# Modulation loaded by quarters, two product groups advancing behind each, index and taps over both row halves

## The chip, the cores and the metric

The kernel runs on one core of one Trainium2 chip, in one launch. The metric is the device time of that core in microseconds (us): median 2101.46 of 3 runs (2100.26 to 2109.39). The core has five engines that run programs of their own and meet by semaphores: TensorE (PE, with its weight loads PEld), VectorE (DVE), ScalarE (ACT), GpSimd (POOL) and SyncE (SP), which here only issues DMAs. TensorE writes to PSUM: two pairs of banks `ps` for the large products, four banks `pm` for everything small.

## The reference, cut to what matters

256 tokens, model width 2048, everything fp32. Two layers follow each other; the change touches the start of the first and two small places.

```
mod = silu(c) @ ada_w + ada_b               # 2048 x 6144: shift, scale, gate
h = rms_norm(x, norm_g) * (1 + scale) + shift
proj = h @ w_in                             # 2048 x 9296: 19 groups of up to 512 columns
q, k = rope(rms_norm(...)); qi, ki = rope(...)        # 16 index heads of 64 channels
score = sum_h relu(qi . ki * 64**-0.5) * wi           # the index; top 64 keys per query
o_a = attention over the selected keys; o_r = gated linear recurrence
x = x + gate * (concat(o_a, o_r) @ w_out)
# second layer: input product, implicit filter (its taps: h3 @ w4, 64 channels deep),
# attention, two branches, output product, feed-forward network
```

`h` depends on the shift and scale of its own channel only: channel tile k (128 channels) of `h` needs columns 128k to 128k+127 of each. No row of `h @ w_in` is complete before all 16 channel tiles are in.

## The kernel before, in words

**The large products.** A weight matrix comes in groups of 512 columns. A group has four chunks (1.049 MB: four channel tiles of 128 x 512 fp32) of two parts each; a part is two channel tiles. Parts are numbered through the whole kernel (`Gemm.part`, L128): group 0 of the input product has parts 0 to 7, group 1 has 8 to 15. For each part ScalarE rounds the weights to `w_hi` (`high`, L390), VectorE subtracts for the remainder `raw_lo` (`low`, L401), and TensorE does 12 matmuls of 512 columns: two channel tiles, two token halves, three products of high and low halves (`multiply_group`, L411). `raw` is a ring of four chunks, `w_hi` a ring of four parts; SyncE issues a chunk when the parts that had its place are multiplied (`stream`, L375). So ScalarE and VectorE can be up to three parts ahead of TensorE. Group j accumulates in bank pair j % 2 of `ps` and must wait until group j - 2 was read out.

**Other work by parts.** Everything else is a generator that yields the part from which it may go on, or the microseconds that a step is guessed to cost (`Spare`, L134). Each engine calls its generators behind each part, some with a budget per part. Constants such as INDEX_AT, GATE_AT and TAPS_AT (L76 to L93) set the parts; ScalarE and VectorE go LEAD = 3 parts behind TensorE's own number, which is about the same moment.

**The modulation.** Shift and scale are 8 groups of 512 columns of ada_w, in order of columns: four groups of shift, four of scale. Each comes in four chunks into the same ring `raw` (SyncE, L2198 to L2203; `ada_free`, L369). TensorE multiplies the column silu(c) with chunks 0 and 2 and one quarter of chunk 3, nine matmuls of 512 columns (`ps<-raw,c_sig`; an fp32 matmul is two instructions in the trace); VectorE multiplies and adds chunk 1 and the rest of chunk 3 into `mod_part` (L1149, L1151), and a matmul with ones adds its partitions (`ps<-mod_part,ones`). ScalarE copies the row to SBUF (L1857), TensorE turns it to columns by four 1x1 products per group (`ps<-ones,mod_row`). When all eight are turned, VectorE makes `mod_cols` and `g_col` (L1163, L1164), ScalarE and VectorE the high and low halves of `h` from the transposed rows (`tile_of_first` L1785 reading the PSUM bank, `low_of_first` L962), and the first product begins. VectorE does small work between its steps in this stretch (`before_products`, L1099): it scales the rows of x, prepares the lower bound of the forget gate (maximum, exponentials, reciprocals) and computes the sines and cosines of the rotation. Three of the eight units of transposes of `hbuf` are made in this stretch, five between the first parts.

**Index and taps.** The index multiplies 16 heads in 8 units j for each token half t (`index`, L642). A unit takes one bank and two matmuls; both read the same 64 partitions, the lower half for even j and the upper for odd j. One unit goes behind each part, from parts 90 and 104 on. ScalarE applies the relu (L1954), VectorE weights and adds (L1268). The taps of the second layer's filter (L756 to L762) are 8 matmuls of 512 columns with 64 partitions, two behind each part; t picks the half, and the first four are t = 0.

Of the kernel before, what the change touches and what calls it, by code (L numbers as in the profile page):

```python
# [9 lines left out]
F32 = mybir.dt.float32  # L10
# [42 lines left out]
ROWS_TURNED = 4  # L53
ADA_PE = 1
# [22 lines left out]
GATE_AT = [12 + 22 * i // 5 for i in range(4 * ADA_GATE)]  # L77
# [28 lines left out]
class Gemm:  # L106


    chunks = 0
    groups_before = 0  # L110

    def __init__(self, sources, k_tiles, groups, columns=None):
        self.sources, self.cpg, self.groups, self.columns = sources, k_tiles // CK, groups, columns
# [14 lines left out]
    def part(self, j, n=0):  # L128
        return self.n0 + self.parts * j + n

# [26 lines left out]
def build(nc, a, out):  # L157
    Gemm.chunks = Gemm.groups_before = 0
    ctx = ExitStack()
    with ctx:  # L160
# [44 lines left out]
        sn_rope = sb("sn_rope", [P, 5, 2 * TT * 96], F32, st)  # L205
        st.close()
# [37 lines left out]
        mod_row = sb("mod_row", [P, 2 * D], F32, st)  # L244
        mod_part = sb("mod_part", [P, 2, GW], F32, st)
# [21 lines left out]
        lb, lb_tmp = proj[:, :, I_Q:I_Q + A_W], xtmp[:].rearrange("p a n -> p (a n)")  # L267
# [48 lines left out]
        mod_bank = ps[1][:, 1]  # L316
# [7 lines left out]
        g_in = Gemm([(w1v, 0)], KT, len(GROUPS_IN), GROUPS_IN)  # L324
# [9 lines left out]
        landed = [sem(f"landed{i}") for i in range(RING)]  # L334
        ada_used = sem("ada_used")
# [29 lines left out]
        def multiplied(eng, gm, j):  # L365
            eng.wait_ge(mm_done, gm.part(j + 1))
            return ps[pair_of(gm, j)]

        def ada_free(sp, g, c):  # L369

            if c != 1:
                sp.wait_ge(ada_used, 3 * (g - 1) + {0: 1, 2: 2, 3: 3}[c])
            if c % 2:
                sp.wait_ge(mod_parts, 2 * (g - 1) + 1 + c // 2)

        def stream(sp, gm, beside=None):

            for j in range(gm.groups):
                for c in range(gm.cpg):
                    k = gm.c0 + gm.cpg * j + c  # L380
                    if k < RING:
                        ada_free(sp, n_ada, k)
                    else:
                        sp.wait_ge(mm_done, PARTS * (k + 1 - RING))
                    v, o = gm.source(j)
                    sp.dma_start(raw[:, k % RING, :, 0:gm.width(j)], v[c][:, :, o:o + gm.width(j)]).then_inc(landed[k % RING], 16)
# [3 lines left out]
        def high(act, gm, j, n):  # L390
# [3 lines left out]
            if p % PARTS == 0:  # L394
                act.wait_ge(landed[k % RING], 16 * (n_ada + k // RING + 1))
# [15 lines left out]
        def multiply_group(pe, gm, j, stat, before=None, beside=None):  # L411

            pair = pair_of(gm, j)
            if gm.g0 + j >= 2:
                evacuated(pe, gm, j - 2)
            kt = gm.cpg * CK
            for n in range(gm.parts):
                if before is not None:
                    before(n)
                p = gm.part(j, n)  # L420
                pe.wait_ge(lo_done, p + 1)
                hi = w_hi[:, p % HRING]
                lo = raw_lo[:, (p // PARTS) % RING, HT * (p % PARTS):HT * (p % PARTS) + HT]
                for i in range(HT):
                    k = HT * n + i
                    x_hi, x_lo = stat(k, j)
                    for t in range(TT):
                        tok = slice(t * P, t * P + P)
                        for q, (l, r) in enumerate(((x_hi, hi), (x_hi, lo), (x_lo, hi))):
                            mm = nc.tensor.matmul(ps[pair][:, t, 0:gm.width(j)], l[:, tok], r[:, i, 0:gm.width(j)],  # L430
                                                  start=(k == 0 and q == 0), stop=(k == kt - 1 and q == 2))
                mm.then_inc(mm_done, 1)
                if beside is not None:
                    beside.step(p)
# [74 lines left out]
        def _(pe):  # L509
# [27 lines left out]
            pe.wait_ge(sig("c_silu"), 1)  # L537
            for g in range(n_ada):
                pe.wait_ge(sig("mod_read"), g + 1)
                for c in (0, 2, 3):  # L540
                    pe.wait_ge(landed[c], 16 * (g + 1))
                    for k in range(CK if c < 3 else ADA_PE):
                        m = mm(ps[g % 2][0:1, 0, :], c_sig[:, CK * c + k:CK * c + k + 1], raw[:, c, k],
                               start=(c == 0 and k == 0), stop=False)
                    m.then_inc(ada_used, 1)
                pe.wait_ge(mod_parts, 2 * g + 2)
                mm(ps[g % 2][0:1, 0, :], ones[:, 0:1], mod_part[:, g % 2], start=False, stop=True).then_inc(sig("mod_sum"), 1)
                if g >= 1:
                    pe.wait_ge(sig("mod_read"), g + 2)
                    for j in range(4 * (g - 1), 4 * g):  # L550
                        mm(mod_bank[:, j:j + 1], mod_row[0:1, j * P:j * P + P], ones[0:1, 0:1])
                if g >= ROWS_TURNED and g < ROWS_TURNED + 3:
                    pe.wait_ge(sig("h1_rows"), 1)
                    turn_unit("h1", hbuf, g - ROWS_TURNED)
            pe.wait_ge(sig("mod_read"), n_ada + 2)
# [1819 lines left out]
```

## Time and profile before

| | |
|---|---|
| runs | 2100.26, 2101.46, 2109.39 us |
| profiled execution | 2106.29 us, span 2104.5 us |
| TensorE busy | 2058.0 us, 98% |
| VectorE, ScalarE, GpSimd busy | 1302.7, 927.1, 383.0 us |
| mean granted TensorE clock | 0.986 of 2.4 GHz |
| DMA | 408.47 MB, mean 194 GB/s; 353 and 344 GB/s in the first two fortieths |

The busy time of TensorE says that it has work in its pipe, not that it is at its peak: ends of matmuls are modelled, so the durations of neighbours overlap; the distance between two starts is what one costs. "Idle before" is the time an engine stood still ahead of an instruction and what ended it. The granted clock is a share of 2.4 GHz; 0.5 is the lower of its two levels.

### The profile page before, as it was taken

The numbers are of one execution on the slowest core, as the hardware profiler recorded it, in microseconds if no ns is written. First come the engines' busy times: TensorE is split into PE (matmuls) and PEld (weight loads), VectorE is DVE, ScalarE is ACT, GpSimd is POOL, SyncE is SP. The second block draws the span as 40 slices with busy tenths as digits, with TensorE's granted clock in tenths as the row PEclk, the third lists the DMA queues.
The fourth block names the chain that finished last, engine by engine and source line by source line (L and its number), as shares of the span: only waits on it lengthen the run. The fifth ranks groups of instructions, "written<-read, shape, count | busy, mean of one in ns | idle before, by whom it ended". The sixth has DMA issues, their size and how long they took to land.

```text
span 2104.5 us, 23568 instructions
## 1 busy us (share of the span) xinstructions
PE 2058.0 (98%) x9245; PEld 1623.4 (77%) x9245; DVE 1302.7 (62%) x1651; ACT 927.1 (44%) x1224; POOL 383.0 (18%) x588
## 2 busy tenths in 40 slices
PE   6989999999999999999999999999999999999999
PEld 1268787777887888786788888888888888878887
DVE  4857667798666678865765666554544544444443
ACT  1165523455654544354454434554444444433332
POOL 0000002999999950000000000000000000000000
PEclk9999989999999999999999999999999999999999
DMA  9967557555565675554435555555555555546554
GB/s 353 344 236 249 199 185 220 180 171 164 171 213 196 200 231 180 160 163 130 138 129 186 187 198 180 180 194 187 191 188 186 194 186 194 194 166 199 186 195 160
DMA packets 205683, 408.47 MB, mean 194 GB/s; under 512 B 10826, under 2 KB 12163, under 8 KB 204931
## 3 DMA queue, kind: packets, MB, share of 16 engines
q1 hardware_dynamic: 190480, 376.07, 54.1%
q10 hardware_dynamic: 13332, 24.40, 3.4%
q0 software_dynamic: 1760, 6.49, 1.5%
q8 instruction: 73, 1.20, 0.2%
q14 instruction: 38, 0.31, 0.0%
HBM read 404.83 MB, written 2.10 MB: 193 GB/s over the span
## 4 chain that ended last, share of the span: by engine, by line
PE 91%; DVE 6%; DMA 2%; issue 1%; ACT 0%; ACTq 0%; SPq 0%; DVEq 0%
PE ps L430 81%; PE pm L511 6%; DMA raw<-in_ada_w 2%; DVE raw_lo L408 1%; PE ps L511 1%; PE pm L523 1%; DVE mod_part L1151 1%; PE pm L575 1%; PE pm L888 0%; DVE gate L1182 0%; DVE xtmp L1351 0%; DVE sc_i L1268 0%; DMA rows_b<-in_hgrn_norm_g 0%; DVE proj L1328 0%; PE pm L710 0%
## 5 line engine op out<-in xcount | busy, mean ns | idle before, releaser
L408 DVE TENSOR_TENSOR raw_lo<-raw,w_hi 128x1024 fp32r<-128x1024 f32 (+1 forms) x648 | 799.9, 1238 | 597.6 <-ACT w_hi L399 589.0
L399 ACT ACTIVATE w_hi<-raw 128x1024 fp32r<-128x1024 f32 (+1 forms) x648 | 680.1, 1050 | 821.0 <-PE ps L430 796.3
L430 PE MATMUL ps<-w_hi,h_hi 128*128 128x512 f32 (+1 forms) x2336 | 941.3, 403 | 12.5 <-DVE raw_lo L408 6.4
L430 PE MATMUL ps<-w_hi,h_lo 128*128 128x512 f32 (+1 forms) x2336 | 912.5, 391 | 0.0
L430 PE MATMUL ps<-raw_lo,h_hi 128*128 128x512 f32 (+1 forms) x2336 | 911.2, 390 | 0.0
L430 PEld LDWEIGHTS ps<-w_hi,h_hi 128*128 128x128 f32 x2336 | 442.8, 190 | 117.3 <-issue 13.0
L430 PEld LDWEIGHTS ps<-raw_lo,h_hi 128*128 128x128 f32 x2336 | 443.3, 190 | 93.3 <-issue 7.7
L430 PEld LDWEIGHTS ps<-w_hi,h_lo 128*128 128x128 f32 x2336 | 442.2, 189 | 93.4
L2265 POOL TENSOR_TENSOR proj<-proj 128x128 f32<-128x128 f32 x264 | 177.8, 679 | 12.9
L2265 POOL TENSOR_TENSOR proj<-proj,w1T 128x128 f32<-128x128 f32 x165 | 102.8, 631 | 11.4 <-DMA proj<-in_z 4.2
L430 PE MATMUL ps<-w_hi,hid_hi 128*128 128x512 f32 x256 | 100.6, 393 | 2.0 <-DVE raw_lo L408 2.0
L430 PE MATMUL ps<-raw_lo,hid_hi 128*128 128x512 f32 x256 | 100.3, 392 | 0.0
L430 PE MATMUL ps<-w_hi,hid_lo 128*128 128x512 f32 x256 | 100.2, 391 | 0.0
L2244 POOL DMA_DIRECT2D proj<-in_z x22 | 14.1, 645 | 344.4 <-DVEq L1246 338.7
L511 PE MATMUL ps<-raw,c_sig 128*1 128x512 f32 x144 | 70.2, 638 | 6.7 <-DMA raw<-in_ada_w 6.5
L430 PEld LDWEIGHTS ps<-w_hi,hid_hi 128*128 128x128 f32 x256 | 48.3, 189 | 12.3 <-DVE raw_lo L408 2.2
L511 PEld LDWEIGHTS ps<-raw,c_sig 128*1 128x1 f32 x144 | 11.5, 87 | 59.5 <-issue 47.0
L430 PEld LDWEIGHTS ps<-w_hi,hid_lo 128*128 128x128 f32 x256 | 48.5, 189 | 10.1
L430 PEld LDWEIGHTS ps<-raw_lo,hid_hi 128*128 128x128 f32 x256 | 48.4, 189 | 10.0
L1182 DVE SCALAR_TENSOR_TENSOR gate<-proj,c_sig,gate 128x512 f32<-128x512 f32 x64 | 49.1, 767 | 1.9
L2265 POOL TENSOR_TENSOR proj<-h3T,proj 128x128 f32<-128x128 f32 x66 | 48.9, 742 | 0.0
L1151 DVE SCALAR_TENSOR_TENSOR mod_part<-raw,c_sig,mod_part 128x512 f32<-128x512 f32 x48 | 36.0, 750 | 10.2 <-DMA raw<-in_ada_w 8.6
(308 smaller groups left out, 1183.5 us busy)
## 6 DMA issues: line engine op xcount, KB each, us to landing
raw<-in_w_in SPq DMA_DIRECT2D x140, 1024.0 KB, 5.2
raw<-in_w_ffn_gate SPq DMA_DIRECT2D x44, 1024.0 KB, 5.2
raw<-in_w_ffn_up SPq DMA_DIRECT2D x44, 1024.0 KB, 5.2
raw<-in_w_ffn_down SPq DMA_DIRECT2D x44, 1024.0 KB, 5.2
raw<-in_ada_w SPq DMA_DIRECT2D x32, 1024.0 KB, 7.7
raw<-in_w_out SPq DMA_DIRECT2D x32, 1024.0 KB, 5.2
proj<-in_ada_w ACTq DMA_DIRECT2D x16, 1024.0 KB, 5.3
raw<-in_w_br_hyena SPq DMA_DIRECT2D x8, 1024.0 KB, 5.2
```

The source lines that it names most:

```text
L399: nc.scalar.activation(w_hi[:, p % HRING, :, 0:gm.width(j)], raw[:, k % RING, e:e + HT, 0:gm.width(j)], ACT.Copy).then_inc(hi_done, 1)
L408: nc.vector.tensor_tensor(raw_lo[:, k % RING, e:e + HT, 0:gm.width(j)], raw[:, k % RING, e:e + HT, 0:gm.width(j)], w_hi[:, p % HRING, :, 0 ...
L430: mm = nc.tensor.matmul(ps[pair][:, t, 0:gm.width(j)], l[:, tok], r[:, i, 0:gm.width(j)], start=(k == 0 and q == 0), stop=(k == kt - 1 and ...
L511: return nc.tensor.matmul(o, l, r, start=start, stop=stop, **kw)
L523: i = nc.tensor.transpose(b[:, ((k % 2) * TT + t) * P:((k % 2) * TT + t + 1) * P], src[:, t, k * P:k * P + P], ident[:])
L575: i = nc.tensor.transpose(b[:, o:o + P], src[:, t, h * HD:h * HD + HD], ident[:])
L1151: i = v.scalar_tensor_tensor(mod_part[:, g % 2], raw[:, c, k], w_, mod_part[:, g % 2], ALU.mult, ALU.add)
L1182: x = v.scalar_tensor_tensor(acc, gate_raw[i % 2][:, k], c_sig[:, CK * c + k:CK * c + k + 1], acc, ALU.mult, ALU.add)
L2244: pool.dma_start(z_k[e % 2][half * HID:half * HID + HID], z.partition_broadcast(HID)).then_inc(sig(f"z_in{e % 2}"), 16)
L2265: g.tensor_tensor(o, x, y, op).then_inc(sig("sum_step"), 1)
```

## The change

1. **Order of ada_w.** The 8 groups are loaded as shift 0, scale 0, shift 1, scale 1, ...: each pair (a quarter) is enough for four channel tiles of `h`. They go to four buffers of their own in `proj`, so `raw` is free for w_in. Behind each odd group's chunks 0 and 1 SyncE issues one chunk of w_in for group 0 and one for group 1.
2. **Who sums.** TensorE now takes chunk 0 and half of chunk 2 (six matmuls), VectorE the other ten steps of sixteen instead of seven. The sums are in banks of `pm`.
3. **Two product groups together.** Parts 0 to 15 alternate between groups 0 and 1 by chunk. Behind quarter q come parts 4q to 4q + 3, worked off while the next quarter is loaded and summed (`early_part`). The last quarter's four come after all.
4. **Transposes.** All 8 units are made ahead of the third group's sums and copied to SBUF (`h1_raw`); `tile_of_first` reads them there.
5. **Moved.** The rotation's angles go from the first stretch to groups 2 and 3 (budget 1.6 per part); the 16 chunks of the gate row start at parts 22 to 78 instead of 12 to 78; the reciprocals are cut in four.
6. **Index and taps.** A unit pair takes two banks, and the four matmuls alternate the halves; the pair stands behind every second part, one part later than the first of the two stood. The taps go in the order n, t.

```diff
-GATE_AT = [12 + 22 * i // 5 for i in range(4 * ADA_GATE)]
+GATE_AT = [22 + 56 * i // 15 for i in range(4 * ADA_GATE)]
...
     def part(self, j, n=0):
+        if self.together and j < 2 and n < self.parts:
+            return self.n0 + 2 * PARTS * (n // PARTS) + PARTS * j + n % PARTS
         return self.n0 + self.parts * j + n
...
+        mod_row = sb("mod_row", [P, 2, GW], F32, st)
+        mod_part = sb("mod_part", [P, 2, GW], F32, st)
...
+        h1_raw = sb("h1_raw", [P, KT, SEQ], F32, st)
...
+        ada_raw = [proj[:, 1, o:o + CK * GW].rearrange("p (k n) -> p k n", k=CK) for o in (A_Q, A_V, R_Q, R_I)]
...
         def ada_free(sp, g, c):
-            if c != 1:
-                sp.wait_ge(ada_used, 3 * (g - 1) + {0: 1, 2: 2, 3: 3}[c])
-            if c % 2:
-                sp.wait_ge(mod_parts, 2 * (g - 1) + 1 + c // 2)
+            if c % 2 == 0:
+                sp.wait_ge(ada_used, 2 * (g - 1) + 1 + c // 2)
+            if c:
+                sp.wait_ge(mod_parts, 3 * (g - 1) + c)
...
+            for g in range(n_ada):
+                o = D * (g % 2) + GW * (g // 2)
                 for c in range(RING):
+                    if g:
+                        ada_free(sp, g, c)
+                    sp.dma_start(ada_raw[c], ada_v[:, CK * c:CK * c + CK, o:o + GW]).then_inc(ada_landed[c], 16)
+                    if g % 2 and c < 2:
+                        load(sp, g_in, c, g // 2)
...
+            def early_part(p):
+                n = 2 * (p // 4) + p % 2
+                pe.wait_ge(sig("first_lo"), n + 1)
+                multiply_part(pe, g_in, p % 4 // 2, n, halves)
             for g in range(n_ada):
+                q = g // 2 - 1
...
+                mods = bank(pe, ("mods", q), "v") if q >= 0 and g % 2 == 0 else None
+                sums = bank(pe, ("mod", g), "a")
+                row_sums(g, 0, CK, sums)
+                if q >= 0:
+                    if g % 2 == 0:
+                        turn_modulation(q, mods)
+                    elif g < n_ada - 1:
+                        early_part(4 * q + 2)
+                row_sums(g, 2, PE_C2, sums)
+                if q >= 0 and g % 2 and g < n_ada - 1:
+                    early_part(4 * q + 3)
+                pe.wait_ge(mod_parts, 3 * g + 3)
+                mm(sums[0:1, :], ones[:, 0:1], mod_part[:, g % 2], start=False, stop=True).then_inc(filled, 1)
+                if q >= 0:
+                    if g % 2 == 0:
+                        early_part(4 * q)
+                        early_part(4 * q + 1)
+                    elif g == n_ada - 1:
+                        early_part(4 * q + 2)
+                        early_part(4 * q + 3)
+            q = n_ada // 2 - 1
+            turn_modulation(q, bank(pe, ("mods", q), "v"))
+            for p in range(2 * g_in.parts - 4, 2 * g_in.parts):
+                early_part(p)
...
-                    for j in range(IDX_H // 2):
-                        yield INDEX_AT[1 + t] + j
+                    for j in range(0, IDX_H // 2, 2):
+                        yield INDEX_AT[1 + t] + j + 1
-                        b = bank(pe, ("ix", t, j), "a")
-                        part = slice(IDX_D * (j % 2), IDX_D * (j % 2) + IDX_D)
+                        b = [bank(pe, ("ix", t, j + r), "a") for r in range(2)]
                         for q in range(2):
-                            m = mm(b[:, q * SEQ:q * SEQ + nk], qiT[part, j // 2 * 2 + q, t * P:t * P + P], kiT[part, 0:nk])
-                        m.then_inc(filled, 1)
+                            for r in range(2):
+                                part = slice(IDX_D * r, IDX_D * r + IDX_D)
+                                m = mm(b[r][:, q * SEQ:q * SEQ + nk], qiT[part, j + q, t * P:t * P + P], kiT[part, 0:nk])
+                                if q:
+                                    m.then_inc(filled, 1)
...
-                    t, n = i // 4, i % 4
+                    t, n = i % TT, i // TT
...
+                for c, k0 in ((1, 0), (2, PE_C2), (3, 0)):
...
+                    if q >= 0 and g % 2 == 0:
+                        if c == 1:
+                            columns_of(q)
+                        else:
+                            low_of_first(2 * q + c - 2)
+                    if g % 2 and c == 3:
+                        for p in range(4 * (g // 2), 4 * (g // 2) + (2 if g == n_ada - 1 else 4)):
+                            low_of(p)
+                    early.step(g, 3.0 if g < 2 else 1.2)
...
+                p = 4 * (g // 2)
+                high_of(p)
+                high_of(p + 1)
+                if g < n_ada - 1:
+                    high_of(p + 2)
+                    high_of(p + 3)
+                read_row(g)
+                act.wait_ge(sig("mod_ready"), g // 2 + 1)
+                for u in (g - 1, g):
+                    tile_of_first(u)
...
-            groups(g_in, range(1, g_in.groups), None, beside)
+            groups(g_in, (2, 3), None, ((chain, 1e9), (angles, 1.6), (gate_work, 1.0)))
+            groups(g_in, range(4, g_in.groups), None, beside)
```

## Rows read from the trace of the kernel before

**Rows 1.** The page, costliest groups: instructions, count, busy, mean, idle before.
```profile
L430 PE MATMUL ps<-w_hi,h_hi 128*128 128x512 f32 (+1 forms) x2336 | 941.3, 403 | 12.5 <-DVE raw_lo L408 6.4
```

**Rows 2.** Chain of waits, first stretch: start, length in us, what.
```profile
98.78 10.45 DMA raw<-in_ada_w
...
135.14 57.15 PE ps L430 x252
```

**Rows 3.** Stages: length, busy us (instructions) per engine, granted clock, DMA share, GB/s.
```profile
60.00:70.00 10.00, 8.99 (x27) 2.14 (x25) 8.73 (x17) 0.59 (x1) 0.00 (x0) 1.00 1.05 388
80.00:90.00 10.00, 8.16 (x24) 3.15 (x23) 9.68 (x11) 0.59 (x1) 0.00 (x0) 0.81 1.02 371
90.00:100.00 10.00, 10.00 (x23) 2.06 (x22) 6.48 (x6) 0.35 (x1) 0.00 (x0) 0.85 0.58 203
120.00:130.00 10.00, 9.39 (x39) 7.63 (x40) 4.63 (x10) 7.12 (x14) 0.00 (x0) 0.81 0.06 8
```

**Rows 4.** Timeline of TensorE: start, us, instruction, count, idle before and what ended it.
```profile
75.37 7.88 PE L511 MATMUL ps<-raw,c_sig 128*1 128x512 f32 x18
...
85.09 1.02 PE L511 MATMUL ps<-mod_part,ones 128*1 128x512 f32 x2 [1.84 <-DVE mod_part L1151]
...
112.65 1.94 PE L511 MATMUL ps<-ones,mod_row 1*128 1x1 f32 x16
...
120.61 0.79 PE L430 MATMUL ps<-w_hi,h_hi 128*128 128x512 f32 x1 [5.43 <-DVE h_lo L967]
...
167.65 0.39 PE L430 MATMUL ps<-w_hi,h_hi 128*128 128x512 f32 x1
```

**Rows 5.** Timeline of VectorE in the first stretch.
```profile
36.90 2.33 DVE L1151 SCALAR_TENSOR_TENSOR mod_part<-raw,c_sig,mod_part 128x512 f32<-128x512 f32 x3 [1.10 <-DMA raw<-in_ada_w]
...
45.98 2.61 DVE L1023 TENSOR_SCALAR hbuf<-x_res,hs 128x2048 f32<-128x2048 f32 x2
...
51.09 1.23 DVE L1113 TENSOR_TENSOR xtmp<-proj 128x1024 f32<-128x1024 f32 x1
...
85.07 3.35 DVE L1126 RECIPROCAL xtmp<-xtmp 128x512 f32<-128x512 f32 x1
...
114.70 0.19 DVE L1163 TENSOR_TENSOR mod_cols<-ps,cols 128x32 f32<-128x32 f32 x1 [3.05 <-PE ps L511]
...
119.80 0.76 DVE L967 TENSOR_TENSOR h_lo<-xtmp,h_hi 128x256 fp32r<-128x256 f32 x2
```

**Rows 6.** Timeline of ScalarE: two of the four activations of one tile pair.
```profile
117.04 0.54 ACT L1793 ACTIVATE xtmp<-pm,mod_cols,g_col 128x256 f32<-128x256 f32 x1
117.49 0.54 ACT L1793 ACTIVATE h_hi<-pm,mod_cols,g_col 128x256 fp32r<-128x256 f32 x1
```

**Rows 7.** VectorE's work on the sines alone, 30 to 82 us: busy, clock, DMA.
```profile
30.00:82.00 52.00, 11.36 (x25) 0.98 1.02 371
```

**Rows 8.** Chain of waits around index and taps.
```profile
424.06 0.64 PE pm L511 x4
424.70 2.95 PE ps L430 x12
...
469.33 1.06 PE pm L511 x4
...
482.43 0.61 ACT proj L1954
...
512.96 1.38 DVE raw_lo L408
...
875.59 1.91 PE pm L511 x4
```

**Rows 9.** Timeline of TensorE: six instructions over both halves, and the next.
```profile
330.01 0.71 PE L511 MATMUL pm<-proj 64*128 64x128 f32 x6
330.65 0.37 PE L511 MATMUL pm<-qaT,kaT 128*32 128x64 f32 x14
```

**Rows 10.** Stage of the index up to where the chain leaves TensorE.
```profile
420.00:482.00 62.00, 62.00 (x269) 47.18 (x269) 53.90 (x87) 35.41 (x77) 57.48 (x87) 1.00 0.55 172
```

More of the change, by code:

```diff
@@ L334, in build @@
         landed = [sem(f"landed{i}") for i in range(RING)]
+        ada_landed = [sem(f"ada_landed{i}") for i in range(RING)]
         ada_used = sem("ada_used")
@@ L419, in multiply_group @@
                     before(n)
[L420 to L432, printed above, removed]
+                multiply_part(pe, gm, j, n, stat)
                 if beside is not None:
-                    beside.step(p)
+                    beside.step(gm.part(j, n))
         def multiply(pe, gm, stat, before=None, beside=None):
@@ L555, in _, with row_sums @@
-            pe.wait_ge(sig("mod_read"), n_ada + 2)
-            for j in range(4 * (n_ada - 1), 4 * n_ada):
-                m = mm(mod_bank[:, j:j + 1], mod_row[0:1, j * P:j * P + P], ones[0:1, 0:1])
-            m.then_inc(sig("mod_turned"), 1)
+            def row_sums(g, c, n, b):
+                pe.wait_ge(ada_landed[c], 16 * (g + 1))
+                for k in range(n):
+                    m = mm(b[0:1, :], c_sig[:, CK * c + k:CK * c + k + 1], ada_raw[c][:, k], start=(c == 0 and k == 0), stop=False)
+                m.then_inc(ada_used, 1)
@@ L735, in _ @@
             beside = Chains(mixer, gate_sum)
-            def turn_h1(n):
-                if n + 3 < KT // 2:
-                    turn_unit("h1", hbuf, n + 3)
-                drained(("h1", n))
-            for j in range(g_in.groups):
-                multiply_group(pe, g_in, j, halves, turn_h1 if j == 0 else None, beside if j else None)
+            for j in range(2, g_in.groups):
+                multiply_group(pe, g_in, j, halves, None, beside)
             multiply(pe, g_o, halves, made("mix"), beside)
@@ new lines, in _ @@
+                    if g % 2 and c == 3:
+                        for p in range(4 * (g // 2), 4 * (g // 2) + (2 if g == n_ada - 1 else 4)):
+                            low_of(p)
+                    early.step(g, 3.0 if g < 2 else 1.2)
+            for p in range(2 * g_in.parts - 2, 2 * g_in.parts):
+                low_of(p)
+            columns_of(n_ada // 2 - 1)
+            for u in (KT // 2 - 2, KT // 2 - 1):
+                low_of_first(u)
+            early.rest()
+            angles = Spare(rotation_angles())
@@ L2035, in _ @@
             beside = ((chain, 1e9), (norm_work, 1.2), (gate_work, 1e9))
-            groups(g_in, range(1, g_in.groups), read_in, None, beside)
+            groups(g_in, range(2, g_in.groups), read_in, None, beside)
             assert norm_work.over and gate_work.over
```

248 lines of the change are left out of this document (131 added, 117 removed).

## The prediction, as put on record before the result

> **What bounds the kernel now.** I read the page first, then the chain of waits, then the timelines of the engines from the start of the span to the third group of the input product. The product's matmuls make up nearly the whole span, and the engine hardly idles before them [rows 1]. So there are only three places where time can be won or lost: the stretch before the first product, places where TensorE's stream carries extra work, and places where VectorE holds TensorE up.
>
> In the first stretch the chain stands on the transfers of ada_w up to 109.23 us (98.78 + 10.45) [rows 2]. The DMA moves 388 GB/s there [rows 3], so one 1.049 MB chunk takes 2.7 us. TensorE is far from full: the row sums of one group (9 chunk rows, 18 instructions) take 7.88 us [rows 4] of the 11 that its four chunks take. After the last chunk VectorE needs 2.3 (three steps, as at 36.90) [rows 5], the turning and reading some 3, columns, splits and tiles the rest: the first product starts at 120.61, the third group at 167.65 [rows 4]. One part (12 matmuls) takes 2.73 us where nothing lies between (252 matmuls in 57.15) [rows 2]. The change can only alter how far 167.65 moves, and what is later.
>
> **The new first stretch.** Eight chunks of w_in join the 32 of ada_w: a quarter of the modulation (two groups) is now 10 chunks, 27 us at 2.7 us each. What it must wait for is longer than that, by my count, because a quarter's work closes a ring over both engines. I follow it from one "ones" matmul of an even group to the next:
> - ones matmul 0.9 (a pair takes 1.02 with its end) [rows 4], two parts 5.46, odd group's first row sums (8 instructions at 7.88/18 = 0.44) 3.5, part 2.73, second row sums (4) 1.75, part 2.73, ones 0.9, next group's first row sums 3.5, turning eight blocks (16 instructions) 1.94 [rows 4]: 23.4 on TensorE.
> - Then TensorE stands still but for 1.75 of row sums: columns 0.45 (0.19, a wait and one like it), tile 1.9 (four activations, 0.45 from start to start, and the end), its low half 0.8, and four steps of chunk 3 at 0.78 = 3.1 [rows 5, 6]: 6.3.
> Sum 29.7 us per quarter, above the 27 of the DMA. TensorE idles 6.3 - 1.75 = 4.6 us in it. What such a stall does to the clock: after 5.43 us without work before 120.61 [rows 4] the granted clock of 120 to 130 is 0.81 [rows 3], 3.8 us at 1.2 GHz instead of 2.4, and 1.9 us are lost; around the 1.84 us before 85.09 [rows 4] it is 0.81 and 0.85 over 20 us [rows 3], 6.8 us at the lower level, 3.4 lost. I take 2.0 per quarter, nearest to the longer stall, bounds 0 and 3.4.
>
> The start: two w_in chunks stand ahead of the second group's last two, so they come 5.4 us later, at 42.4 (before, VectorE's step on the last began at 36.90 [rows 5]). In between VectorE scales x (2.85) and takes a maximum (1.2) [rows 5]: it is done at about 48.4. Then eight units of transposes at 0.6, 4.8; row sums 3.5, turning 1.94, and the 6.3 from above, with the ones matmul and waits between them: the third group's ones matmul at 66.0. Two quarters follow: 66.0 + 2 x (29.7 + 2.0) + 1.7 for reciprocals in the second (512 columns take 3.35, so 256 about 1.7) [rows 5] = 131.1. The rest is ones 0.9, lower clock 2.0, parts 5.46, row sums 5.25, a wait for the last chunk 0.4, ones 0.9, parts 5.46, turning 1.94, then columns, tile and low half 3.5 with nothing to multiply: 156.9. Four parts 10.9 and 1.6 for the clock after that stall give **169.4 against 167.65: 1.8 us lost**. So moving 12 parts (33 us) ahead buys nothing but what the 8 chunks (21.6) and the ring over the engines take back. Bounds: without any loss by clock (7.6) 5.8 won; at 3.4 in each of the three quarters 4.2 more lost.
>
> Nothing else stands in the way of the third group: chunk 8 of w_in waits for part 9 alone, long done, and ScalarE has 5.5 us (parts 14 and 15) for one high half and the read of the first group, before the third group writes that bank. Both are costed at nothing; if the read were late it would be one instruction, about 1 us.
>
> **The rotation angles move to groups 2 and 3.** In before they lie under the DMA, 11.36 us of them [rows 7] and some 1.3 of the small products that feed them, an estimate. Now parts 16 to 23 hold eight low halves and four forget-gate steps, all of 1024 columns like the maximum at 51.09, 1.23 each (14.7), the angles (12.7) and two parts of gate row, each two steps like the modulation's at 0.78 (3.1): 30.5 us of VectorE against 8 x 2.73 = 21.8 of TensorE. VectorE runs up to three parts ahead, 8.2 us, less 2.3 for a high and a low half: 5.9. 30.5 - 21.8 - 5.9 = **2.8 lost**. Bounds 0 (if the slower first stretch leaves VectorE more lead) and 5. The gate row's 16 chunks now lie in parts 22 to 78 instead of 12 to 78, denser by 0.13 us a part, where VectorE has a stretch that holds TensorE up already; 0.5 for that (0 to 2).
>
> **Index and taps.** A narrow unit of the index takes 0.64 and the part behind it 2.95 instead of 2.73: 0.86 in all. The wide unit takes 1.06 and two taps 1.91, and the parts behind them are as long: 1.28 and 2.13 [rows 8]. The four instructions of each have 128, 256 and 512 columns; that the step from 128 to 256 adds 0.42 and that to 512 another 0.85 makes 0.43, 0.85 and 1.70 of them streaming. So every break of the stream costs 0.43 beside its own columns. Sixteen breaks become eight. Do halves run side by side? The recurrence's six instructions over two halves of 128 columns end in the time that four take in one half: 330.01 to 330.65, 0.64 us [rows 9], like the narrow unit [rows 8]. So yes, as far as six instructions can show it. Pairs then save 0.43 + 0.32 to 0.43 (narrow), 0.43 + 0.64 to 0.85 (wide), and each pair of taps 0.43 to 0.85. The lower numbers come if the first half-pass has nothing beside it.
>
> The Trainium skill, "TensorE: Matmul & The Clock Gate", Part 3, says that matmuls start and end strictly in program order even when they sit in different rows. With eight instructions ordered two by two this would give five slots of eight, the lower numbers; the recurrence's row above is nearer to full overlap. By the page a pair of taps saves 0.43 and all four save 1.7 instead of 3.4.
>
> But not all of it reaches the end. From 482.43 the chain leaves TensorE and goes through VectorE until 514.3 (512.96 + 1.38) [rows 8]: what TensorE saves after that is lost. Before 482, four narrow pairs save 4 x 0.8 = 3.2 and two wide ones 2 x 1.2 = 2.4: 5.6. VectorE must follow: it is idle for 8.1 of the 62 us from 420 to 482 [rows 10], so there is room, and I take **5.6 won** (bounds 0, if it doesn't follow, and 8.5). Taps: the chain is on TensorE all through [rows 8]; **2.6 won** (0 to 3.4).
>
> **Sum.** 1.8 + 2.8 + 0.5 - 5.6 - 2.6 = -3.1 us. The profiled execution took 2106.29 with a span of 2104.5, the median of the runs is 2101.46; taken off the median: **2098.4 us**.
>
> **Rivals.**
> 1. The clock never falls, and VectorE enters the third group with enough lead. For it: between 60 and 70 us TensorE was busy for 8.99 of 10 us and the clock stayed at 1.00 [rows 3], and the parts make the new stretch denser than that but for the one stall. Against it: that stall is 4.6 us. It gives 2098.4 - 7.6 - 2.8 - 0.4 = 2087.6. Chance 0.25.
> 2. Slower: the clock stays low after each stall for the whole quarter's first leg, and again in its odd group, since row sums and turns fill TensorE less than parts. Price 3.4 twice instead of 2.0 once, 4.8 more in each of three quarters: 14.4, so 2112.8. It decides from 3.0 us lost per quarter on, where the gain of 3.1 is gone. For it: the 6.8 us at the lower level around a stall of only 1.84. Against it: parts are dense work. Chance 0.13.
> 3. Index doesn't pay: VectorE is nearly full there [rows 10] and takes its steps by parts, each now a part later; the 5.6 vanish and 2104.0 is left. If the halves don't overlap at all, 2.6 of it stay by the eight breaks saved and the taps give 0: nearly the same time. This is also the case in which the change doesn't do what it says. Chance 0.12.
> The forecast has 0.5, with its own range 2091 to 2106.
>
> **Chances.** What a measurement of this kernel can tell is about 0.5%, 10.5 us: faster means under 2091.0, slower over 2112.0. Rival 1 lies mostly beyond the first bound (0.22), the forecast's tail adds 0.05: 0.27. Half of rival 2 and tails of the others: 0.15. The rest is 0.58. The range leaves out the far halves of rivals 1 and 2: 2086 to 2113.
>
> **What would show it.** Parts 0, 4 and 8 some 32 to 34 us apart, with TensorE idle for 4 to 5 us before the ones matmul of groups 2, 4 and 6, waiting for VectorE and not for a DMA; a granted clock under 1.0 right after; the third group at 165 to 174. A stall of 2 to 4 us at parts 21 to 23, released by a low half. Index pairs of eight instructions in 0.85 to 1.1 us more than a bare part (narrow) and 1.3 to 1.5 (wide); the chain still on VectorE at the end of the index. It is wrong if the third group starts before 162 or after 178, if quarters follow each other at 27 us (then the DMA bounds them), or if the low halves never keep TensorE waiting before part 30.

## The result and the profile after

The changed kernel takes 2112.27 us (median of 16 runs, 2108.85 to 2116.73); the kernel before, on the same chips, 2104.11 (16 runs, 2098.67 to 2109.39). The ratio is 1.0039, 95% interval 1.0028 to 1.0049: **8.2 us slower** (5.9 to 10.3). The forecast was 3.1 us faster. The time lies inside the stated range, but the sign is wrong.

The profiled execution of the changed kernel took 2109.80 us with a span of 2108.0, only 3.5 us more than that of before. The two profiles understate the difference, as the last table of this section shows. The forecast of 2098.4 us stood on a median of three runs, 2101.46; with sixteen it is 2104.11. That the time lies inside the range, by 0.7 us at its upper end, and close to the 2112.8 of rival 2, is luck: the sum behind it is another, as shown below.

The page after, its share of busy engines and the row that answers to [rows 1]:

```profile
PE 2032.2 (96%) x9197; PEld 1614.8 (77%) x9197; DVE 1319.1 (63%) x1683; ACT 932.6 (44%) x1232; POOL 381.7 (18%) x588
L436 PE MATMUL ps<-w_hi,h_hi 128*128 128x512 f32 (+1 forms) x2336 | 943.0, 404 | 20.2 <-DVE raw_lo L419 15.8
```

The first matmuls of the parts now find TensorE idle for 20.2 us instead of 12.5, and 15.8 of them end with a low half of VectorE instead of 6.4. Next the timeline of TensorE in the first stretch (start, length, instruction, count, idle before and what ended it). It shows the ones matmuls of the even groups, the last part's start and the stall in the third group; [rows 4] are those of before.

```profile
50.02 1.87 PE L525 MATMUL pm<-mod_part,ones 128*1 128x512 f32 x2 [5.37 <-DVE mod_part L1209]
51.82 5.35 PE L581 MATMUL pm<-ident,hbuf 128*128 128x128 f32 x32
...
69.19 1.86 PE L525 MATMUL pm<-mod_part,ones 128*1 128x512 f32 x2 [4.79 <-DVE mod_part L1209]
...
101.37 1.87 PE L525 MATMUL pm<-mod_part,ones 128*1 128x512 f32 x2 [4.72 <-DVE mod_part L1209]
103.16 0.80 PE L436 MATMUL ps<-w_hi,h_hi 128*128 128x512 f32 x1
103.76 0.63 PE L436 MATMUL ps<-raw_lo,h_hi 128*128 128x512 f32 x1
...
135.65 1.86 PE L525 MATMUL pm<-mod_part,ones 128*1 128x512 f32 x2 [5.91 <-DVE mod_part L1209]
...
162.00 0.80 PE L436 MATMUL ps<-w_hi,h_hi 128*128 128x512 f32 x1 [3.71 <-DVE h_lo L1012]
...
197.96 0.50 PE L436 MATMUL ps<-w_hi,h_hi 128*128 128x512 f32 x1 [2.98 <-DVE raw_lo L419]
```

(`mod_part,ones` is the matmul with ones that adds VectorE's part of the sum and closes a quarter; `raw_lo` and `h_lo` are low halves.) Every quarter closes as foreseen, over VectorE: TensorE stands idle 4.7 to 5.9 us and is released by VectorE's sum, not by a DMA. After each of these stalls the ones pair takes 1.86 us instead of 1.02 and the first matmuls 0.63 instead of 0.39: they run at the 1.2 GHz level. The stages say the same (length, busy time and instructions of PE, PEld, DVE, ACT and POOL, granted clock, DMA share, GB/s):

```profile
69.20:101.40 32.20, 27.48 (x93) 13.08 (x94) 20.84 (x31) 9.34 (x14) 0.00 (x0) 0.92 0.88 325
101.40:135.60 34.20, 28.34 (x92) 13.64 (x92) 26.79 (x34) 12.53 (x16) 0.00 (x0) 0.90 0.88 319
135.60:162.00 26.40, 22.65 (x80) 12.94 (x80) 17.40 (x23) 8.32 (x12) 0.00 (x0) 0.89 0.58 206
```

The DMA, full in before while ada_w was loaded (1.02 to 1.05 in [rows 3]), is used for 0.88 of the first two quarters. What VectorE did before the ones matmul at 101.37 is in its timeline:

```profile
94.95 0.17 DVE L1188 TENSOR_TENSOR mod_cols<-pm,cols 128x8 f32<-128x8 f32 x1 [1.25 <-PE pm L525]
95.15 0.16 DVE L1191 SCALAR_TENSOR_TENSOR g_col<-mod_cols,cols 128x4 f32<-128x4 f32 x1
95.23 1.53 DVE L1209 SCALAR_TENSOR_TENSOR mod_part<-proj,c_sig,mod_part 128x512 f32<-128x512 f32 x2
97.53 0.76 DVE L1012 TENSOR_TENSOR h_lo<-xtmp,h_hi 128x256 fp32r<-128x256 f32 x2 [0.77 <-ACT h_hi L1854]
98.20 3.11 DVE L1209 SCALAR_TENSOR_TENSOR mod_part<-proj,c_sig,mod_part 128x512 f32<-128x512 f32 x4
```

Nothing in this list waits for a transfer. VectorE waits for the turned blocks (the columns stand ahead of two steps that don't need them), then for ScalarE's tile, and then it does the four steps that TensorE waits for. (In the odd groups it does wait for transfers, 3.33 us before 77.57 for the longest, but TensorE has parts to multiply then.)

The chain of waits (start, length, what) in the index and at the taps, which answers to [rows 8]:

```profile
438.55 0.69 PE pm L525 x8
...
439.69 0.59 DVE sc_i L1329
...
471.04 1.23 DVE raw_lo L419
...
472.32 11.20 PE ps L436 x48
483.52 1.06 PE pm L525 x8
...
520.07 1.31 DVE raw_lo L419
...
885.71 1.06 PE pm L525 x4
886.76 2.96 PE ps L436 x12
```

Eight narrow instructions take 0.69 us instead of twice 0.64, eight wide ones 1.06 instead of twice 1.06, four of the taps 1.06 instead of 1.91. So TensorE saves what was forecast and a little more. But the chain leaves TensorE at 439, directly behind the first pair, and not at 482.

Where the offset of the two profiles arises (start times in us, from the same instructions in both):

| instruction | before | after | offset |
|---|---|---|---|
| first matmul of the third group | 167.65 | 175.76 | 8.1 |
| first matmul on the indicator (ind) | 192.1 | 205.1 | 13.0 |
| last of the recurrence (qaT) | 339.1 | 350.6 | 11.5 |
| first scores behind the index (kT) | 540.9 | 552.9 | 12.0 |
| first on dft, behind the taps | 942.0 | 945.6 | 3.6 |
| span | 2104.5 | 2108.0 | 3.5 |

The first row needs care, because the profiles of before differ there themselves. Before and four kernels of the experiments below have the same first stretch, and their third group starts at 167.65, 164.64, 170.37, 165.66 and 170.64 us. In the changed kernel and three with its first stretch (a_noindex, a_noangles, a_spread) it is 175.76, 175.74, 174.82 and 174.62. So the first stretch does lose; between the two medians it is 7.6 us, and single pairs give 4.0 to 11.1.

3.4 of the 8.4 between kT and dft are the taps (first to last h3T: 16.4 before, 13.0 after), 1.9 arise between kT and the first tap (this way takes 332.7 to 336.5 us in the thirteen profiles, with no order that follows the edits), and 3.1 behind the last one. There one stage differs; here it is before and after in turn (columns as above).

```profile
925.00:945.00 20.00, 20.00 (x88) 16.47 (x87) 8.67 (x15) 5.74 (x10) 0.00 (x0) 0.83 0.42 123
```

```profile
925.00:945.00 20.00, 20.00 (x106) 17.14 (x105) 11.41 (x13) 10.40 (x24) 0.00 (x0) 1.00 0.50 158
```

The same instructions, which the change doesn't touch, ran at a mean clock of 0.83 in one execution and 1.00 in the other. The kernel with the paired index alone has 0.83 there too, the one with spare matmuls 1.00. It goes either way from profile to profile. The sixteen runs of the kernel before alone spread over 10.7 us (2098.67 to 2109.39). So the ends of two single profiles say little about a few us; the offsets are read from stage to stage, and the verdicts from the medians.

### The profile page after: what moved, and what is told of

It reads as the page before. It is cut to its first block, busy times and chain, and to the rows that moved or that the text cites. A ratio compares the mean times of both kernels' runs of the same rounds, so it can differ in the third digit from the quotient of the medians.

```text
span 2108.0 us, 23528 instructions
## 1 busy us (share of the span) xinstructions
PE 2032.2 (96%) x9197; PEld 1614.8 (77%) x9197; DVE 1319.1 (63%) x1683; ACT 932.6 (44%) x1232; POOL 381.7 (18%) x588
## 4 chain that ended last, share of the span: by engine, by line
PE 89%; DVE 8%; DMA 2%; issue 1%; ACT 1%; SPq 0%; ACTq 0%; DVEq 0%
PE ps L436 79%; PE pm L525 7%; DVE raw_lo L419 2%; DMA proj<-in_ada_w 2%; DVE mod_part L1209 1%; PE pm L537 1%; DVE sc_i L1329 1%; DVE xtmp L1412 1%; PE pm L624 1%; PE pm L934 0%; DVE gate L1243 0%; DVE proj L1420 0%; PE pm L581 0%; ACT w_hi L410 0%; DVE proj L1389 0%
## 5 line engine op out<-in xcount | busy, mean ns | idle before, releaser
L436 PE MATMUL ps<-w_hi,h_hi 128*128 128x512 f32 (+1 forms) x2336 | 943.0, 404 | 20.2 <-DVE raw_lo L419 15.8
L2350 POOL TENSOR_TENSOR proj<-proj 128x128 f32<-128x128 f32 x264 | 185.4, 707 | 12.9
L2350 POOL TENSOR_TENSOR proj<-proj,w1T 128x128 f32<-128x128 f32 x165 | 97.6, 600 | 11.1 <-DMA proj<-in_z 3.9
L1209 DVE SCALAR_TENSOR_TENSOR mod_part<-proj,c_sig,mod_part 128x512 f32<-128x512 f32 x72 | 53.9, 749 | 12.8 <-DMA proj<-in_ada_w 10.8
L525 PE MATMUL pm<-proj,c_sig 128*1 128x512 f32 x96 | 48.2, 645 | 10.1 <-DMA proj<-in_ada_w 10.1
L436 PEld LDWEIGHTS ps<-raw_lo,hid_hi 128*128 128x128 f32 x256 | 48.4, 189 | 10.1
L436 PEld LDWEIGHTS ps<-w_hi,hid_lo 128*128 128x128 f32 x256 | 48.4, 189 | 10.0
L525 PEld LDWEIGHTS pm<-proj,c_sig 128*1 128x1 f32 x96 | 7.4, 87 | 43.3 <-issue 33.3
```

The source lines that it names most:

```text
L525: return nc.tensor.matmul(o, l, r, start=start, stop=stop, **kw)
L1209: i = v.scalar_tensor_tensor(mod_part[:, g % 2], ada_raw[c][:, k], w_, mod_part[:, g % 2], ALU.mult, ALU.add)
L2350: g.tensor_tensor(o, x, y, op).then_inc(sig("sum_step"), 1)
```

## The experiments

**Index and taps alone.** The kernel before with each of these two edits by itself, and the changed kernel with the old index.

```diff
-for j in range(IDX_H // 2):                 # one unit, one half
+for j in range(0, IDX_H // 2, 2):           # two units, halves in turn   (b_index; undone in a_noindex)
...
-t, n = i // 4, i % 4
+t, n = i % TT, i // TT                      # b_taps
```

> The kernel before with the index pairs alone (two banks, halves in turn, one part later). Theory A, VectorE sets the pace there and takes its steps one part later: 0 to 1 us either way (in the changed kernel the offset was 11.8 us before the index and 12.0 behind it). Rival, the forecast: TensorE's saving reaches the end up to where the chain left it, 5.6 us faster. The chain should leave TensorE earlier than at 482 us by theory A.

> The kernel before with the taps alone in the order n, t. If halves overlap fully as in the changed kernel's rows (1.06 instead of 1.91 us a pair): 4 x 0.85 = 3.4 us faster. Rival, one half-pass has nothing beside it: 1.7. This should beat both kernels.

> The changed kernel with the old index. Theory A: the same time as the changed kernel, 0 to 1 us either way, so about 1.004 of before. Rival (the pairs did save 5.6 us and the first stretch lost more than its rows show): 5.6 us slower than the changed kernel, about 1.0065.

Measured: b_index 1.0001 (0.9988 to 1.0015), b_taps 0.9999 (0.9985 to 1.0014), a_noindex 1.0060 (1.0042 to 1.0079; six runs). In the traces the way from the last qaT to the first kT is 201.8 us before, 201.3 in b_index, 202.3 after and 201.9 in a_noindex: in these traces the index edit moves nothing in either kernel. TensorE's own saving is there: from the first to the last matmul of the index it is 74.0 us in before and 66.3 in b_index. It turns into waits for low halves. TensorE's waits between qaT and kT, before and then b_index (what for, us in total, times, longest):

```profile
PE ps L430 <- DVE raw_lo L408: 5.5, 6, 1.7
```

```profile
PE ps L430 <- DVE raw_lo L408: 11.6, 7, 4.6
```

6.1 us more, and the chain leaves TensorE at 424 us, as expected. In the changed kernel it is 12.0 us of such waits against 5.7 in a_noindex.

By its median a_noindex misses its expectation: 1.0060 is nearer the rival's 1.0065 than 1.004. Its six runs stand in two clusters, 2112.0 to 2112.7 and 2117.1 to 2117.4, and its interval overlaps that of the changed kernel between 1.0042 and 1.0049. So whether the pairs are worth some 4 us in the changed kernel is open by the medians; no row of the two traces shows it but the stage at 925 to 945, where a_noindex has the clock of 0.83. The taps in b_taps, one row of the tile h3T (duration min, median, max in ns; first and last start):

```profile
L511 PE MATMUL pm<-gate,h3T x16: 589/641/693, 879.8 to 892.7; 64*128 64x512 f32 x16
```

and in before:

```profile
L511 PE MATMUL pm<-gate,h3T x16: 589/589/693, 875.5 to 891.9; 64*128 64x512 f32 x16
```

From first to last start 12.9 us instead of 16.4. The trace shows the saving. The timing doesn't: its interval, 3 us to either side of nothing, leaves out the expected 3.4 by a hair, and this profile is the slowest of the kernel's twelve runs, with 170.64 us at the third group.

**Does VectorE set the pace of the index?** If it does, the pairs must pay once VectorE has less to do. Both kernels below leave out the rotations of the queries and keys on VectorE.

```diff
-                            rotate_gained(heads(proj, c0)[:, t, h:h + 4], x, t)    # b_light
```

b_light_index is b_light with the paired index.

> The kernel before; VectorE's gained rotation of queries and keys (eight times four instructions) is left out. It takes 27 us off VectorE in the stretch of the index and the groups behind it. By theory A the chain then stays on TensorE there and the stretch from the first to the last index matmul (74.0 us) shrinks by 1 to 3. This run is the base of the next.

> The same with the index pairs. Theory A, VectorE's load swallowed the gain: with that load away the pairs save 7 to 8.5 us against b_light (from the last matmul of the recurrence to the first of the attention). Rival, pairs save little on TensorE itself, or one part of delay costs what they save: under 2 us.

Measured: 0.9973 (0.9960 to 0.9986) and 0.9947 (0.9923 to 0.9970), medians 2098.36 and 2091.60. The rows of the tiles qaT and kT in b_light:

```profile
L511 PE MATMUL pm<-qaT,kaT x128: 196/219/314, 283.4 to 343.5; 128*32 128x64 f32 x64, 128*32 128x32 f32 x64
L511 PE MATMUL pm<-kT,qT x32: 270/325/378, 542.5 to 593.6; 128*128 128x128 f32 x16, 128*128 128x256 f32 x16
```

and in b_light_index:

```profile
L511 PE MATMUL pm<-qaT,kaT x128: 196/219/314, 278.6 to 335.6; 128*32 128x64 f32 x64, 128*32 128x32 f32 x64
L511 PE MATMUL pm<-kT,qT x32: 270/325/378, 525.9 to 577.0; 128*128 128x128 f32 x16, 128*128 128x256 f32 x16
```

542.5 - 343.5 = 199.0 us against 525.9 - 335.6 = 190.3: the pairs save 8.7 us where VectorE has room, and nothing (201.8 and 201.3) where it hasn't. By the medians they save 6.8. With the rotations gone the waits for low halves are 3.6 us without and 3.5 with the pairs. Both index edits take VectorE's steps one part later, and here that costs nothing visible, so the delay alone isn't the cause. Nor is GpSimd, which is busy for 92 to 93 of 100 us in the two stages below and for 80.4 of 86 in before. One expectation missed: in b_light alone the index takes 73.8 us, and not 1 to 3 less than 74.0. The stages from 428 to 528 of the two (b_light first) say why: VectorE is busy for 72 to 73 of 100 us.

```profile
428.00:528.00 100.00, 100.00 (x439) 77.02 (x438) 72.33 (x121) 57.10 (x108) 92.44 (x148) 1.00 0.55 174
```

```profile
428.00:528.00 100.00, 99.26 (x478) 79.67 (x477) 73.19 (x121) 59.45 (x108) 92.67 (x145) 1.00 0.59 186
```

In the kernel before it was already nearly full in the like stages:

```profile
439.00:482.00 43.00, 43.00 (x184) 32.87 (x184) 38.96 (x67) 25.32 (x54) 40.20 (x60) 1.00 0.58 177
439.00:525.00 86.00, 84.13 (x364) 64.32 (x364) 79.32 (x133) 46.38 (x89) 80.39 (x117) 1.00 0.55 169
```

and in the changed kernel TensorE, not VectorE, is the one that is idle:

```profile
438.50:524.00 85.50, 77.45 (x359) 60.10 (x359) 79.84 (x132) 42.33 (x77) 79.81 (x119) 0.97 0.56 174
```

**Angles.** The changed kernel without the sines and cosines, and then with them spread over three groups instead of two.

```diff
-                yield from sine(sn_rope, flat, flat, 2 * TT * 96, ...)     # a_noangles
...
-            groups(g_in, (2, 3), None, ((chain, 1e9), (angles, 1.6), (gate_work, 1.0)))
+            groups(g_in, (2, 3, 4), None, ((chain, 1e9), (angles, 0.6), (gate_work, 1.0), (head_work, 1.2)))   # a_spread
...
-            groups(g_in, range(4, g_in.groups), None, beside)
+            groups(g_in, range(5, g_in.groups), None, beside)
```

> The changed kernel without the sine and cosine evaluation (the arguments are used in their place; the five small products stay). In the changed kernel part 23 waits 2.98 us for its low half, and its matmuls then run at the lower clock, 1.9 more. If the angles are the cause, both go: part 16 to 24 in 24.5 us instead of 29.4, 4.9 us faster than the changed kernel. If the gate row or the forget-gate steps are the cause, most of the stall stays.

> The changed kernel with the angles at a budget of 0.6 a part over groups 2 to 4 instead of 1.6 over 2 and 3. If the stall before part 23 comes from the angles' density, nothing waits there: from part 12 to part 24's end 38.3 us as without angles instead of 43.2, 4.9 us faster. Rival, VectorE lacks the room anyway beside gate row and forget-gate steps: a later stall gives most of it back.

Measured: 1.0029 (1.0018 to 1.0040) and 1.0023 (1.0010 to 1.0035). From part 12 to the indicator the changed kernel takes 205.15 - 162.00 = 43.15 us. In a_noangles:

```profile
161.03 0.79 PE L436 MATMUL ps<-w_hi,h_hi 128*128 128x512 f32 x1 [3.71 <-DVE h_lo L1012]
...
199.30 3.63 PE L525 MATMUL pm<-ind,proj 128*128 128x2 f32 x32
```

38.27, and 38.0 in a_spread (161.08 to 199.1), without any stall. The angles cost 4.9 us where they stood: the stall of 2.98 and the 1.9 that the clock behind it took. Stages of the changed kernel at and behind the stall:

```profile
175.70:198.00 22.30, 19.32 (x86) 15.62 (x85) 21.56 (x30) 14.10 (x13) 0.00 (x0) 1.00 0.81 283
198.00:205.30 7.30, 7.30 (x27) 5.88 (x27) 7.12 (x9) 2.66 (x3) 0.00 (x0) 0.77 0.20 53
```

VectorE is busy for 21.56 of 22.3 us, then the clock is 0.77. By the medians the two kernels win 2.1 and 3.4 us on the changed one, less than 4.9, and their intervals overlap its own. The 4.9 are shown by the traces alone.

**The ring of a quarter.** Two ways to shorten TensorE's wait. a_reorder moves VectorE's columns behind one more step of the modulation, and both low halves behind them; a_fill gives TensorE spare matmuls to do in the gap (five in each even group, four behind the last turn; their results are read by nothing).

```diff
-                        if c == 1:
+                        if c == 2:
                             columns_of(q)
-                        else:
-                            low_of_first(2 * q + c - 2)
+                        elif c == 3:
+                            low_of_first(2 * q)
+                            low_of_first(2 * q + 1)                           # a_reorder
```

```diff
                 row_sums(g, 2, PE_C2, sums)
+                if spare is not None:
+                    for k in range(5):
+                        m = mm(spare[0:1, :], c_sig[:, k:k + 1], x_res[:, 0, 0:GW])    # a_fill
```

> The changed kernel; VectorE makes the columns behind chunk 2's steps and both low halves behind chunk 3's four steps, so the ones matmul no longer waits for tile and low half. Theory B, the ring over both engines sets the quarter's length (32.2 and 34.3 us): the ring is some 3 us shorter, TensorE's idle time ahead of the ones matmul falls from 4.7 to 1.5 to 2 us and with it part of the clock's loss; quarters of 28 to 30 us, then close to the DMA's 27; third group 7 to 11 us earlier. Rival, the transfers bound the quarters already (DMA share 0.88): under 2 us.

> The changed kernel with matmuls that nobody needs (five of 512 columns from x into a bank of their own) in TensorE's idle time of each quarter, four in the last one. Theory C, the stall costs clock: ones matmul and two parts behind it run at the higher level; they take 6.4 instead of 8.1 to 9.0 us, and the last first part 2.7 instead of 5.5: 6 to 9 us faster in all than the changed kernel. Rival, the clock falls for another reason: no gain or up to 3 us lost by matmuls that last longer than the stall.

Measured: 1.0008 (0.9994 to 1.0022) and 1.0009 (0.9995 to 1.0023). Timeline of TensorE in a_reorder:

```profile
63.03 1.02 PE L525 MATMUL pm<-mod_part,ones 128*1 128x512 f32 x2 [1.74 <-DVE mod_part L1209]
...
92.82 1.02 PE L525 MATMUL pm<-mod_part,ones 128*1 128x512 f32 x2 [2.15 <-DVE mod_part L1209]
...
125.94 1.86 PE L525 MATMUL pm<-mod_part,ones 128*1 128x512 f32 x2 [7.11 <-DVE mod_part L1209]
...
151.59 0.79 PE L436 MATMUL ps<-w_hi,h_hi 128*128 128x512 f32 x1 [3.71 <-DVE h_lo L1012]
```

Part 12 comes 10.4 us earlier than after. The first two waits shrink to 1.7 and 2.2 us, and the ones pairs behind them run at full clock. The first of the two quarters takes 29.8 us, inside the 28 to 30 expected, the second 33.1, outside. The DMA now is at its limit (share 0.99 and 1.02 in the two stages below), and the chain of waits goes over a transfer:

```profile
90.70 13.27 DMA proj<-in_ada_w
```

From 104.07 to 125.90 it then stays on VectorE, which hardly pauses there: its sums of the next chunks, four low halves and three reciprocals of 1.75 us stand in one row. So the third wait, 7.11 us, is a late start by the DMA and a full VectorE behind it.

```profile
70.00:100.00 30.00, 27.85 (x100) 13.49 (x100) 22.78 (x34) 12.88 (x17) 0.00 (x0) 1.00 0.99 359
100.00:130.00 30.00, 22.89 (x75) 9.82 (x73) 26.68 (x34) 7.82 (x13) 0.00 (x0) 0.89 1.02 372
```

a_fill keeps the order of the ring:

```profile
68.69 1.02 PE L525 MATMUL pm<-mod_part,ones 128*1 128x512 f32 x2 [0.49 <-DVE mod_part L1219]
...
99.42 1.02 PE L525 MATMUL pm<-mod_part,ones 128*1 128x512 f32 x2 [0.42 <-DVE mod_part L1219]
...
131.35 1.02 PE L525 MATMUL pm<-mod_part,ones 128*1 128x512 f32 x2 [1.62 <-DVE mod_part L1219]
...
156.46 0.50 PE L436 MATMUL ps<-w_hi,h_hi 128*128 128x512 f32 x1 [0.18 <-DVE h_lo L1022]
```

Quarters of 30.7 and 31.9 us instead of 32.2 and 34.3, part 12 at 156.46 instead of 162.00 (5.5 earlier) and the indicator at 197.1 instead of 205.1 (8.0 earlier). The ones matmul and the two parts behind it take 6.6 us up to the next row sums, instead of 8.1 to 9.0. The work that it adds is useless; what it wins is the clock.

By the medians a_reorder and a_fill are 6.5 and 6.3 us faster than the changed kernel, and their intervals lie wholly under its own. That is less than the 10.5 and 8.0 at the indicator. 4.7 us of each are gone by the end of the recurrence, 3.2 of them within it: it takes 60.1 us from first to last qaT in these two profiles and 56.9 in the changed kernel's.

**Together.** a_best is a_reorder with a_spread. a_best_fill adds spare matmuls to it: two in the first quarters, five in the third, four behind the last turn. Index pairs and taps are in both.

> The changed kernel with a_reorder's order in VectorE and the spread angles. The two gains lie one behind the other, so they add: third group's matmuls of the forget gate at 190 us instead of 205.1, 15 us faster than the changed kernel and 5 to 7 us faster than before (ratio 0.997).

> a_best with spare matmuls in the idle time that is left (two per quarter, five in the third, four in the last). Theory C: the last stall no longer costs 2.7 us of clock nor the third quarter's 1.7; 3 to 5 us faster than a_best, ratio 0.995 to 0.996 of before. If the spare matmuls outlast the stall: no gain.

Measured: 0.9986 (0.9972 to 0.9999) and **0.9966 (0.9954 to 0.9979)**, median 2097.84: 7.1 us less than the kernel before (4.4 to 9.7) and the fastest of the kernels that compute everything. Both fall somewhat short of what was expected: the indicator of a_best comes at 189.9 (190 expected), but the ratio is 0.9986 and not 0.997; the spare matmuls give 2.7 us by the medians and not 3 to 5, and the two intervals overlap. The timeline of TensorE in a_best_fill:

```profile
126.46 1.02 PE L525 MATMUL pm<-mod_part,ones 128*1 128x512 f32 x2 [2.77 <-DVE mod_part L1219]
...
152.09 0.50 PE L436 MATMUL ps<-w_hi,h_hi 128*128 128x512 f32 x1 [0.18 <-DVE h_lo L1022]
...
187.63 3.63 PE L525 MATMUL pm<-ind,proj 128*128 128x2 f32 x32
```

In the third quarter 2.8 us of waiting are left, and six matmuls behind them still take 0.63 us. The indicator comes at 187.6, 17.5 us earlier than after and 4.5 earlier than in the profile of before (189.1 to 195.1 in the five kernels with the old first stretch). At kT 3.5 us are left of it; the taps add 3.4, and the span is 7.0 us shorter.

## Why the prediction was wrong, step by step

1. **The quarter's ring: right as a mechanism, undersized.** The parts 0, 4 and 8 follow each other at 32.2 and 34.3 us (31.7 and 33.4 foreseen), TensorE idles 4.7 to 5.9 before the ones matmul, released by VectorE. But the third group starts at 175.8 instead of 169.4, and 8.1 us are lost instead of 1.8 (7.6 by the medians of five and four profiles). The 6.4 are: the start 3.2 (the first ones matmul at 69.19, not 66.0: VectorE is ready for the second group's at 50.02 instead of 48.4, that pair runs at the low clock, the transposes take 5.35 instead of 4.8, and the idle time is 4.8 long); the two quarters 1.4; the last one 0.5; and 1.3 in the four parts behind it, since the whole first part ran at 1.2 GHz (5.50 us in the chain instead of the 2.73 of [rows 2]; 1.6 had been put down for it). The 2.0 us of clock per quarter were well sized: 1.4, 2.4 and 2.3, against a_fill. Of the two rows that they were taken from, the one with 6.8 us at the lower level after a wait of 1.84 was chance: in b_index the same wait, 1.83 us, is followed by a clock of 1.00 from 80 to 100 us.
2. **Angles: the wait was right, its clock forgotten.** The stall came at part 23, released by a low half, as foreseen, 2.98 us long (2.8). The 1.9 us at the lower clock behind it were counted for the first stretch and left out here: 4.9 lost.
3. **Gate row:** nothing to be seen of the 0.5: from the indicator to the last of the recurrence the offset shrinks from 13.0 to 11.5, with the chance of the clock in the recurrence in it.
4. **Index: this is the step whose mechanism failed.** "VectorE must follow: it is idle for 8.1 of the 62 us from 420 to 482 [rows 10], so there is room, and I take **5.6 won**". By the traces it gives 0. VectorE's idle time was taken as room. Half of the 8.1 us lay ahead of 439; behind it VectorE was busy for 38.96 of 43 us, and what was left to it were waits in a fixed order: when TensorE is done sooner, its next parts need their low halves sooner, and these stand behind the same index and rotation steps. In the changed kernel the chain goes through exactly these from 439.69 to 472.27, and TensorE idles for 8.0 of the 85.5 us from 438.5 to 524 (1.9 of 86 before). Rival 3 held in its first half, VectorE's load, as b_light and b_light_index show: the same edit wins 8.7 us where VectorE has less to do.
5. **Taps:** 3.4 won instead of 2.6. The halves overlap in full: four instructions over two halves and the longer part behind them add 1.06 + 2.96 - 2.73 = 1.29 us, which is the 0.43 of a break and 0.86, half of the 1.70 that the prediction had for the columns of four in one half.

The Trainium skill, "TensorE: Matmul & The Clock Gate", Part 3, had been weighed there for its rule that matmuls start and end in program order. Together with an order two by two, which was an assumption, it gave 1.7 us for the four taps instead of 3.4. The traces don't agree with that estimate: they show 12.9 and 13.0 for 16.4, and the four instructions of a pair of taps start at 885.635, 885.642, 886.168 and 886.175 us, so both halves begin within 7 ns. In which order they stand in the program isn't in the trace, so no run here decides on the rule itself.

Corrected sum: 8.1 + 4.9 + 0 + 0 - 3.4 = 9.6 us, against 8.2 measured (5.9 to 10.3). Of the forecast's error of 11.3 (8.2 + 3.1), 6.3 are the first stretch, 5.6 the index, 2.1 the angles' clock, less 0.8 for the taps, 0.5 for the gate row and 1.4 that the sum leaves over. With a gain of only 3.1 forecast, the first stretch alone (6.3) or the index alone (5.6) would have turned the sign. None of the rivals was it alone. Rival 3 came true and had been priced by itself. Rival 2, the clock, came true at the last part alone (2.7 us lost instead of 1.6), not in the quarters for which it was priced.

**Open.** Why the granted clock falls in some executions in the stage at 925 to 945 us, and for a longer or shorter time in the recurrence (first to last qaT 56.9 to 60.1 us in the profiles), isn't known; nor why the old first stretch ends anywhere from 164.6 to 170.6 us. The index pairs were not taken out of the fastest kernel, so whether they give it anything isn't shown. The taps' 3.4 us and the angles' 4.9 are shown by the traces alone. That VectorE's fixed order, and not its load alone, holds TensorE up in the index is argued from the chain; no run changes the order there.

## What to carry to other kernels

A saving on one engine counts only where another doesn't set the pace (5.6 us forecast for the index, none seen in the traces): compare the second engine's work with the stage's new, shorter length, and not with the old one. Where work is cut into pieces that feed each other, follow the ring over all engines and give the engine that is waited for first what doesn't depend on the late result (10.4 us here, by an order of four lines). Price each stall on TensorE with the lower clock behind it (1.4 to 2.7 us for each stall of 3.0 to 5.9 here); where the stall can't go, spare matmuls in the gaps won 8.0 us at the indicator, 6.3 by the medians.

## What the runs showed of the hardware

Matmuls that alternate between the two row halves overlap fully, at every width met here: eight of 128 columns in 0.69 us against twice 0.64, eight of 256 in 1.06 against twice 1.06, and four of 512 in 1.06 against 1.91.

After each idle time of 3.0 to 5.9 us in the changed kernel's first 200 us the matmuls that followed ran at 1.2 GHz (0.63 us for 0.39), and after the 3.71 us before 162.00, with only the turning of small blocks ahead of it, for a whole part. Short waits go both ways. Behind the 1.74 us before 63.03 in a_reorder the ones pair still runs at full clock, then eight matmuls take 0.58 to 0.63, and the granted clock from 60 to 70 is 0.83; behind the 2.77 us before 126.46 in a_best_fill it is the same, with six of 0.63. Behind the 2.15 before 92.82 in a_reorder the clock stays at 1.00, and so it does behind the 1.62 before 131.35 in a_fill. The same wait in the same code gives either: 1.84 us in before, then 0.83 from 80 to 100 us; 1.83 us in b_index, then 1.00.
